# Adaptive norms of a second transformer stack, taken by row tile: factors multiplied in by a product with their diagonal, and the next sublayer's first products started on tile 0

## The chip, the cores and the metric

One core of a Trainium2 chip runs the whole program in one launch. The metric is the device time of that launch in microseconds (us), as the median of three runs. TensorE is called PE in the profile, VectorE DVE, ScalarE ACT, GpSimd POOL, and SyncE (which issues the loads) SP.

## The reference

Two stacks of transformer layers run one after the other on one sequence of 256 tokens and 1024 features, in fp32. The first stack (two layers of f1, m, f2, with plain norms) ends in a norm of its own. The second stack (two layers of F1, M, F2) is the one at issue. Its norms are "adaptive": each of the six sublayers has a shift, a scale and a gain of its own, computed from a condition vector.

```python
def _rms_norm(x, g):
    y = x * lax.rsqrt(jnp.mean(x * x, axis=-1, keepdims=True) + 1e-6)
    return y * g

def _modulate(x, shift, scale):
    return x * (1.0 + scale) + shift

# second stack, layer l: F1, M, F2
n = _modulate(_rms_norm(h, norm_g[l, 0]), sh1, sc1)
h = h + 0.5 * ga1 * _swiglu(n, ffn_w_in[l, 0], ffn_w_out[l, 0])
n = _modulate(_rms_norm(h, norm_g[l, 1]), sh2, sc2)
h = h + ga2 * _token_mixing(n, ...)
n = _modulate(_rms_norm(h, norm_g[l, 2]), sh3, sc3)
h = h + 0.5 * ga3 * _swiglu(n, ffn_w_in[l, 1], ffn_w_out[l, 1])
# after both layers
return _rms_norm(h, final_norm_g)
```

The mean of squares runs over the 1024 features of a token. So the factor of a token (its row) is known only when both 512-column halves of its row of x are complete.

## The kernel before

**Tiles.** The 256 tokens are two row tiles of 128 (tile 0 and tile 1, `t` in the code), and x is `m.x[:, t, :]`, tokens on the partitions. A product needs the features on the partitions, so x is turned by PE, 128x128 at a time (`turn_x`, L1484), and kept as a high and a low part, `xh` and `xl`. Each weight block is split the same way: ACT rounds it into `wh` (L1755), DVE subtracts to get `wl` (L1999). A product of full accuracy is then three PE products: xh with wh (L1509), xh with wl (L1510), xl with wh (L1512), each 128x512. A "sub" is two 128-row blocks of a weight, so it is 12 products for the two tiles. There are five buffers for split subs (`NH`), three are kept ahead (`LA`), and four raw buffers take the loads. SP issues the load of a raw buffer after the last DVE split of the one that it replaces (`load`).

**Order.** Each engine's instructions are generated by the same walk through one `Order` class, in program order per engine; semaphores tie them. There is no planner. What stands first in the walk stands first in each queue.

**The end of a sublayer.** `into_x` computes the down (or output) projection into x, by halves of 512 columns (`h`). In the last half the two last subs are done by `tail`: 12 products (L1523 to L1525) for tile 0, then 12 for tile 1. DVE multiplies the sum by the gain row `gaB` (L2089) and adds it to x (L2091), ACT squares and sums (`square_part`, L1775). In the FFNs the first half of x is turned 8 products into the second half's work (`prep` at k = 4), in the output projection of M between the two tails.

**The norm of the second stack.** `leave` waits for the squares of both tiles, `scale_part` forms the mean on DVE (L2039, L2041), POOL takes it to the power -1/2 for both tiles at once (`rr`, L2392). Meanwhile the rest of x is turned and multiplied by the feature's factor (`v_hi` on ACT L1789, `v_lo` on DVE L2055). DVE makes `dg`, the diagonal of the token factors (L2063), PE spreads it over all partitions by a product with ones (`spread_rr`, L1552), and then for each of 8 feature blocks DVE multiplies `vT` by the spread factors (L2070), ACT adds the shift into `xh` (L1796), and DVE forms `xl` (L2075). Only then do the next sublayer's products start (`gemm_sub`), both tiles together.

The six places where this happens are called T1 to T6 here: T1 is the entrance to the second stack, after the first stack's final norm (`final`, L2379, and `enter`), then T2 = F1 to M, T3 = M to F2, T4 = F2 to F1, T5 = F1 to M, T6 = M to F2. At the end of all, `final` scales x and `store` writes it out.

Of the kernel before, what the change touches and what calls it, by code (L numbers as in the profile page):

```python
# [12 lines left out]
P = 128  # L13
D = 1024
# [68 lines left out]
LA = 3  # L83
AGE = 3
# [256 lines left out]
class Signals:  # L341
    def __init__(self, sem):
# [6 lines left out]
        self.pow = Sem(sem("s_pow"), "POOL")  # L349
# [19 lines left out]
class Order:  # L369
# [5 lines left out]
    def __init__(self, k, e, count):  # L375
# [3 lines left out]
        self.sub_of = {}  # L379
# [12 lines left out]
        self.set_up = False  # L392

# [188 lines left out]
    def prep_hi(self, p, nx):  # L582
        for n, (k, b, tk) in enumerate(p):
            if nx[0] == "plain":
                done = self.new(self.s.act, "xh")
                self.x_hi_plain(k, b, tk, nx, done)
                self.x_hi[k] = self.x_hi[k + 1] = done
            elif n == 0:
                self.need_ada(nx[1], 4)
                done = self.new(self.s.act, "v")  # L590
                self.v_hi(k, b, tk, nx[1], done)
                self.free[b] = self.v_at[k // 2] = done
# [4 lines left out]
    def v_hi(self, k, b, tk, s, done):  # L597
        pass

    def prep_lo(self, p, nx):  # L600
        for n, (k, b, tk) in enumerate(p):
            if nx[0] == "plain":
                done = self.new(self.s.vec, "xl")
                self.x_lo_plain(k, b, nx, self.x_hi[k], done)
                self.free[b] = self.x_lo[k] = self.x_lo[k + 1] = done
            elif n == 1:
                done = self.new(self.s.vec, "v")
                self.v_lo(k, b, tk, nx[1], done)
                self.free[b] = self.v_at[k // 2] = done
# [4 lines left out]
    def v_lo(self, k, b, tk, s, done):  # L614
        pass

    def finish(self, nx):
        s = nx[1]
        b = self.next_t()
        self.spread_rr(s, b)  # L620
        for k in range(9):
            if k < 8:
                self.shifted_hi(s, k, b)
            if k > 0:
                self.shifted_lo(s, k - 1)
# [4 lines left out]

    def spread_rr(self, s, b):
        pass

    def shifted_hi(self, s, k, b):
        pass

    def shifted_lo(self, s, k):
        pass

    def enter(self, nx):  # L640
        mod = nx[0] == "mod"
        if mod:
            for h in range(2):
                for t in range(2):
                    self.square(t, h)
            self.row_scale()
        self.prep(0, nx)
        self.prep(1, nx)
        if mod:
            self.finish(nx)  # L650
        self.ahead()
        if not mod:
            for h in range(2):
                for t in range(2):
                    self.square(t, h)
            self.row_scale()

    def leave(self, nx, bb):
        if nx is not None and nx[0] == "plain":
            p = self.prep_turn(1, bb)  # L660
            self.prep_hi(p, nx)
            self.prep_lo(p, nx)
            self.square(1, 1)
            self.row_scale()
            return
# [18 lines left out]
    def into_x(self, label, banks2, X, K, ready, ga, nx, hook, start=None, td=None):  # L684
        turned, p = nx is None, None
        for h in range(2):
            b, k = start[h] if start else (banks2(), 0)
            end = K if h == 0 else max(k, K - 4)
            while k < end:
# [3 lines left out]
                if h == 1 and k == 4 and not turned:  # L693
                    self.prep(0, nx)
                    turned = True
            if h == 0:
# [7 lines left out]
                continue  # L704
            two = [self.take(label) for _ in range((K - k) // 2)]
            self.ahead()
            for t in range(2):
# [1848 lines left out]
```

## Time and profile before

| | |
|---|---|
| median of 3 runs | 2398.83 us (2398.77 to 2399.57) |
| the profiled execution | 2399.14 us, its span 2397.1 us |
| PE busy | 2283.8 us (95%), 10872 instructions |
| DVE busy | 1578.8 us (66%) |
| ACT busy | 1130.4 us (47%) |
| POOL busy | 19.7 us (1%), 26 instructions |
| mean granted PE clock | 0.981 |

The span runs from the first to the last instruction, and the execution takes 2.0 us more than it. "Busy" of PE is modelled and overlaps (a 128x512 product is shown with 0.39 us and the next starts 0.23 us later), so 95% is not 95% of what PE can do. The granted clock is 1.00 when TensorE runs at its full 2.4 GHz and 0.50 at 1.2 GHz.

### The profile page before, as it was taken

What the parts mean: (1) busy time and instruction counts of PE and PEld (TensorE: products, weight loads), DVE (VectorE), ACT (ScalarE), POOL (GpSimd) and SP (SyncE); (2) the same over time, 40 slices, a digit from 0 to 9 for tenths busy, and PEclk for the clock granted to TensorE, in tenths of its full rate; (3) what the DMA queues carried; (4) which work ended last, traced back from release to release, by engine and by line L of the source; (5) the groups of instructions that cost most, each with busy time, mean ns of one, the idle gap of its engine ahead of it and who ended that gap; (6) DMA issues with size and microseconds to landing.
All of it is one profiled execution on the core that took longest, in us unless ns stands there. A gap on an engine that the chain in (4) does not pass through costs nothing.

```text
span 2397.1 us, 27023 instructions
## 1 busy us (share of the span) xinstructions
PE 2283.8 (95%) x10872; PEld 1903.9 (79%) x10872; DVE 1578.8 (66%) x2391; ACT 1130.4 (47%) x1707; POOL 19.7 (1%) x26
## 2 busy tenths in 40 slices
PE   7999899999999899989999999899999999998998
PEld 6888778888888788868887877788787778777887
DVE  4556775555557669967985545689689955447565
ACT  4445444444444444454444555444444445554443
POOL 0000000000000000000000000000000000000000
PEclk9999999999999999989999999999999999998999
DMA  7554445555554358847874433488589844335563
GB/s 256 192 186 150 124 128 196 176 193 177 201 175 125 121 187 296 294 162 264 305 261 141 128 123 123 158 298 293 199 282 304 290 139 137 123 106 180 199 209 123
DMA packets 250385, 462.91 MB, mean 193 GB/s; under 512 B 9543, under 2 KB 55537, under 8 KB 250133
## 3 DMA queue, kind: packets, MB, share of 16 engines
q1 hardware_dynamic: 250020, 461.04, 57.6%
q8 instruction: 85, 1.39, 0.2%
q14 instruction: 40, 0.32, 0.0%
q10 hardware_dynamic: 240, 0.16, 0.0%
HBM read 460.12 MB, written 1.05 MB: 192 GB/s over the span
## 4 chain that ended last, share of the span: by engine, by line
PE 73%; DVE 13%; issue 9%; ACT 3%; POOL 0%; DMA 0%; ACTq 0%; DVEq 0%; POOLq 0%
PE ps L1509 15%; PE ps L1512 15%; PE ps L1510 15%; PE s L1512 6%; PE s L1509 5%; PE s L1510 5%; DVE wl L1999 4%; PE ps L1484 3%; DVE acc L2007 3%; DVE cacc L2185 2%; PE s L1570 2%; PE ps L1590 1%; ACT wh L1755 1%; PE ps L1525 1%; PE ps L1523 1%
## 5 line engine op out<-in xcount | busy, mean ns | idle before, releaser
L1999 DVE TENSOR_TENSOR wl<-raw,wh 128x1024 fp32r<-128x1024 f32 (+1 forms) x748 | 861.7, 1176 | 397.0 <-ACT wh L1755 391.9
L1755 ACT ACTIVATE wh<-raw 128x1024 fp32r<-128x1024 f32 (+1 forms) x748 | 742.7, 1019 | 342.3 <-PE ps L1512 235.5
L1509 PE MATMUL ps<-wh,xh 128*128 128x512 f32 (+3 forms) x1728 | 671.9, 389 | 18.3 <-DVE wl L1999 11.8
L1512 PE MATMUL ps<-wh,xl 128*128 128x512 f32 (+3 forms) x1728 | 654.5, 379 | 0.0
L1510 PE MATMUL ps<-wl,xh 128*128 128x512 f32 (+3 forms) x1728 | 654.1, 379 | 0.0
L1509 PEld LDWEIGHTS ps<-wh,xh 128*128 128x128 f32 x1728 | 329.4, 191 | 92.3 <-DVE wl L1999 17.8
L1512 PEld LDWEIGHTS ps<-wh,xl 128*128 128x128 f32 x1728 | 329.0, 190 | 53.1 <-DVE xl L2075 0.4
L1510 PEld LDWEIGHTS ps<-wl,xh 128*128 128x128 f32 x1728 | 330.0, 191 | 48.9
L2007 DVE SCALAR_TENSOR_TENSOR acc<-raw,condT,acc 128x512 f32<-128x512 f32 x252 | 189.3, 751 | 7.7
L1509 PE MATMUL s<-wh,xh 128*128 128x512 f32 x384 | 150.3, 391 | 1.9 <-DVE wl L1999 1.9
L1512 PE MATMUL s<-wh,xl 128*128 128x512 f32 x384 | 149.6, 390 | 0.0
L1510 PE MATMUL s<-wl,xh 128*128 128x512 f32 x384 | 149.4, 389 | 0.0
L1509 PE MATMUL s<-wh,hTh 128*128 128x512 f32 x352 | 138.5, 393 | 0.0
L1512 PE MATMUL s<-wh,hTl 128*128 128x512 f32 x352 | 137.3, 390 | 0.0
L1510 PE MATMUL s<-wl,hTh 128*128 128x512 f32 x352 | 137.2, 390 | 0.0
L1761 ACT ACTIVATE ach<-acc 128x512 fp32r<-128x512 f32 x36 | 22.7, 632 | 211.0 <-DVE acc L2007 199.0
L2111 DVE TENSOR_TENSOR hTl<-ps,hTh 128x512 fp32r<-128x512 f32 x88 | 56.9, 685 | 94.8 <-ACT hTh L1812 94.8
L1812 ACT ACTIVATE hTh<-ps 128x512 fp32r<-128x512 f32 x88 | 48.3, 593 | 141.7 <-PE ps L1484 141.6
L1509 PE MATMUL ps<-wh,hTh 128*128 128x512 f32 x288 | 112.6, 391 | 0.0
L1512 PE MATMUL ps<-wh,hTl 128*128 128x512 f32 x288 | 112.1, 389 | 0.0
L1510 PE MATMUL ps<-wl,hTh 128*128 128x512 f32 x288 | 112.0, 389 | 0.0
L1819 ACT ACTIVATE pt<-pt,small 128x128 f32<-128x128 f32 (+1 forms) x88 | 42.0, 478 | 141.5 <-DVE small L2119 141.5
(311 smaller groups left out, 2480.1 us busy)
## 6 DMA issues: line engine op xcount, KB each, us to landing
raw<-in_ffn_w_in SPq DMA_DIRECT2D x80, 1024.0 KB, 5.3
raw<-in_ada_w SPq DMA_DIRECT2D x72, 1024.0 KB, 5.2
raw<-in_ffn_wg SPq DMA_DIRECT2D x40, 1024.0 KB, 5.2
raw<-in_ffn_wu SPq DMA_DIRECT2D x40, 1024.0 KB, 5.2
raw<-in_ffn_wd SPq DMA_DIRECT2D x40, 1024.0 KB, 5.2
raw<-in_ffn_w_out SPq DMA_DIRECT2D x40, 1024.0 KB, 5.3
raw<-in_mix_w_in SPq DMA_DIRECT2D x28, 1024.0 KB, 5.1
raw<-in_w_in SPq DMA_DIRECT2D x28, 768.0 KB, 4.5
```

What stands on the lines that cost most here:

```text
L1484: return self.e.transpose(out, src, self.m.ident[0:n, 0:n])
L1509: e.matmul(o, X[0](kk, t), hi, start=kk == 0, stop=False)
L1510: e.matmul(o, X[0](kk, t), lo, start=False, stop=False)
L1512: ins = e.matmul(o, X[1](kk, t), hi, start=False, stop=kk == K - 1)
L1570: ins = self.e.matmul(m.s45[:, o:o + w], q, k, start=True, stop=True)
L1755: ins = self.e.activation(m.wh[j % NH][:, 0:n], m.raw[u % NR][:, k0 * w:k0 * w + n], ACT.Copy)
L1812: self.then_inc(self.e.activation(m.hTh[:, k:k + 2, :].rearrange("p k s -> p (k s)"), m.ps[b], ACT.Copy), th)
L1819: self.then_inc(self.e.activation(d, d, ACT.Exp, bias=st.sm[:, t:t + 1], scale=-1.0, accum_out=st.sm[:, 4 + t:5 + t]), sgm["exp"])
L1999: ins = self.e.tensor_tensor(m.wl[j % NH][:, 0:n], m.raw[u % NR][:, k0 * w:k0 * w + n], hi, ALU.subtract)
L2007: ins = self.e.scalar_tensor_tensor(out=a, in0=m.raw[u % NR][:, k * 512:k * 512 + 512], scalar=m.condT[:, kk:kk + 1], in1=a if kk else m.b ...
L2111: self.then_inc(self.e.tensor_tensor(lo, m.ps[b], hi.bitcast(F32), ALU.subtract), tl)
L2185: ins = e.scalar_tensor_tensor(out=a, in0=src, scalar=w, in1=a, op0=ALU.mult, op1=ALU.add)
```

## The change

1. The tail takes three subs instead of two where x leads to an adaptive norm or to a final norm (`TAIL`), so 18 products for tile 0, then 18 for tile 1. After M the tail stays at two subs.
2. Each tile has a norm of its own: squares, `scale_part` (one DVE instruction in place of two, the division by 1024 now sits in the scale of the square) and the power on POOL run for one tile.
3. x isn't turned by a transpose and multiplied afterwards. `scaled_part` multiplies a 128x128 block of x with the tile's `dg`, which turns it and applies the token's factor in one plain fp32 product. Eight such products per tile; no spread, no `L2070`.
4. The feature's factor and the shift are applied together while PSUM is read, per 128x128 block: to `xh` directly (ACT) and to `vT` (ACT or DVE), then `xl` is `vT` minus `xh`.
5. `skewed` runs the first 8 x 2 blocks (four subs) of the next sublayer's first projection by tile: tile 0's 24 products, with tile 1's gain, add, squares, norm and turn beside or between them, then tile 1's 24 products.
6. Four subs must be split before the norm. One of the low parts is taken by POOL (`split_lo_pool`), on a semaphore of its own.
7. The transposes in the FFN's second half and between M's tails go away. The first stack's final norm and the last one also go by tile, and each tile is stored on its own.

```diff
+TAIL = 3
...
+    def lower(self, pool=False):
+        j, u, k0, nk, w, last = self.later.pop(0)
+        if pool:
+            self.lo_at[j] = (self.s.plo, j)
+            self.split_lo_pool(j, u, k0, nk, w)
+        else:
+            self.lo_at[j] = (self.s.lo, j)
+            self.split_lo(j, u, k0, nk, w)
+        if last:
+            self.load(u + NR, self.lo_at[j], self.lo_at[j - 1] if k0 else None)
...
+    def skewed(self, label, banks):
+        nx, add_1 = self.half
+        s = nx[-1]
+        while self.wsub < self.taken + 4:
+            self.make(later=True)
+        v0 = self.turn_scaled(s, 0, (self.next_t(), self.next_t()))
+        add_1(lambda: self.shifted_v(s, 0, 2, v0))
+        self.shifted_hi(s, 0, 0, v0)
+        self.shifted_hi(s, 0, 1, v0)
+        self.square(1, 1)
+        if len(self.later) > 1:
+            self.lower()
+        self.lower(pool=True)
+        self.shifted_v(s, 0, 3, v0)
+        self.shifted_hi(s, 0, 2, v0)
+        self.shifted_hi(s, 0, 3, v0)
+        self.normed(1, nx)
+        self.shifted_v(s, 0, 0, v0)
+        self.shifted_v(s, 0, 1, v0)
+        js = [self.take(label) for _ in range(4)]
+        x = {k: (s, 0, k // 2) for k in range(8)}
+        self.first_hi(js, banks[0], x)
+        self.shifted_lo(s, 0, 2)
+        if nx[0] == "mod":
+            v1 = self.turn_scaled(s, 1, (4, 5))
+        for p in (0, 1, 3):
+            self.shifted_lo(s, 0, p)
+        self.first_lo(js, banks[0], x)
+        if nx[0] == "final":
+            v1 = self.turn_scaled(s, 1, (4, 5))
...
+        self.first_rest(js, banks[1])
+        self.ahead()
...
-            end = K if h == 0 else max(k, K - 4)
+            end = K if h == 0 else max(k, K - (4 if plain else 2 * TAIL))
...
+    def scaled_part(self, s, t, bb, tk):
+        m = self.m
+        self.wait_ge(*(self.xr[t, h] for h in range(2)), (self.s.vec, ("dg", s, t)))
+        for k in range(8):
+            b = bb[k // 4]
+            self.wait_ge(self.free[b])
+            ins = self.e.matmul(m.ps[b][:, (k % 4) * P:(k % 4 + 1) * P], m.x[:, t, k * P:(k + 1) * P],
+                                m.dg[:, t * P:(t + 1) * P], start=True, stop=True)
+            if k % 4 == 3:
+                self.then_inc(ins, tk[k // 4])
...
+    def split_lo_pool(self, j, u, k0, nk, w):
...
+        ins = self.e.tensor_tensor(m.wl[j % NH][:, 0:n], m.raw[u % NR][:, k0 * w:k0 * w + n], hi, ALU.subtract)
+        self.then_inc(ins, (s.plo, j))
```

PE at T2, before: the last product of tile 1's tail, the transposes of x's second half, the spread of the factors, and the first products of M's first projection (`wh` and `xh` are high parts).

```order
L1525 MATMUL ps<-wh_61,hTl 128x512
L1484 MATMUL s<-cst,x 128x128 [waits s_vec]
L1484 MATMUL s<-cst,x 128x128 x3
L1484 MATMUL s<-cst,x 128x128 [waits s_vec]
L1552 MATMUL ps<-dg,cst 128x256 [waits s_act,s_vec]
L1509 MATMUL ps<-wh_57,xh 128x512 [waits s_act]
L1510 MATMUL ps<-wl_62,xh 128x512
L1512 MATMUL ps<-wh_57,xl 128x512 [waits s_vec]
```

PE at T2, now: tile 1's last product, the scaled turn of tile 0 (L1651), tile 0's products with `xh` (L1664, L1667, L1671), the scaled turn of tile 1, tile 0's products with `xl` (L1683) and tile 1's (L1694 and on).

```order
L1621 MATMUL ps<-wh_61,hTl 128x512
L1651 MATMUL ps<-dg,x 128x128 [waits s_vec]
L1651 MATMUL ps<-dg,x 128x128 x7
L1664 MATMUL ps<-wh_57,xh 128x512 [waits s_act,s_hi]
L1664 MATMUL ps<-wh_59,xh 128x512 [waits s_act]
L1664 MATMUL ps<-wh_60,xh 128x512 [waits s_act]
L1671 MATMUL ps<-wl_64,xh 128x512 [waits s_lo]
L1651 MATMUL s<-dg,x 128x128 [waits s_vec]
L1683 MATMUL ps<-wh_57,xl 128x512 [waits s_vec]
L1681 MATMUL ps<-wl_65,xh 128x512 [waits s_plo]
L1683 MATMUL ps<-wh_60,xl 128x512 [waits s_vec]
L1694 MATMUL ps<-wh_57,xh 128x512 [waits s_act]
```

The spread is gone, the products with `xh` stand ahead of those with `xl`, and the second tile's turn stands between them.

DVE at T2, now: from tile 0's gain to tile 1's diagonal.

```order
L2232 TENSOR_TENSOR ps<-ps,gaB_75 128x512 [waits s_prod]
L2241 TENSOR_TENSOR x<-ps,x 128x512 [waits s_vec]
L2195 SCALAR_TENSOR_TENSOR ms<-ssq 128x1 [waits s_act]
L2210 TENSOR_SCALAR dg<-cst,rr 128x128 [waits s_pow]
L2232 TENSOR_TENSOR ps<-ps,gaB_75 128x512 [waits s_sub]
L2219 TENSOR_SCALAR vT<-ps,Gc_83,shc_81 128x128 [waits s_turned]
L2241 TENSOR_TENSOR x<-ps,x 128x512 [waits s_vec]
L2155 TENSOR_TENSOR wl_64<-raw_56,wh_59 128x1024 [waits s_hi]
L2219 TENSOR_SCALAR vT<-ps,Gc_83,shc_81 128x128 x2
L2195 SCALAR_TENSOR_TENSOR ms<-ssq 128x1 [waits s_act]
L2227 TENSOR_TENSOR xl<-vT,xh 128x2x128 [waits s_act,s_vec]
L2210 TENSOR_SCALAR dg<-cst,rr 128x128 [waits s_pow]
```

Before, both gains and adds stood in a row and one mean, one power and one pair of diagonals followed. Now tile 1's gain and add stand behind tile 0's diagonal, with a read of tile 0's turned x between them.

POOL, now, around T1 and T2 (two powers per tile at T1, since the final norm takes one too).

```order
L2549 TENSOR_TENSOR rr<-ms,cst 128x2 [waits s_vec]
L2549 TENSOR_TENSOR rr<-ms,cst 128x1 [waits s_vec] x2
L2543 TENSOR_TENSOR wl_64<-raw_54,wh_59 128x1024 [waits s_hi]
L2549 TENSOR_TENSOR rr<-ms,cst 128x1 [waits s_vec] x3
L2543 TENSOR_TENSOR wl_65<-raw_56,wh_60 128x1024 [waits s_hi]
```

Before, POOL's queue here held powers alone. Now the split of a sub stands between tile 0's power and tile 1's, six times in all.

## Rows read from the trace of the kernel before

**Rows 1.** Stretches: us, busy of PE, PEld, DVE, ACT, POOL, granted clock, DMA share
```profile
1057.50:1070.60 13.10, 5.07 (x19) 3.26 (x18) 6.53 (x16) 5.74 (x16) 1.39 (x2) 0.65 0.01 1
1070.60:1075.50 4.90, 4.90 (x12) 3.88 (x13) 4.83 (x13) 3.33 (x8) 0.00 (x0) 0.54 0.00 0
1263.30:1269.20 5.90, 1.94 (x11) 1.06 (x9) 3.55 (x9) 1.97 (x6) 0.69 (x1) 1.00 0.71 187
1269.20:1273.40 4.20, 4.16 (x11) 3.22 (x12) 4.18 (x12) 2.84 (x6) 0.00 (x0) 0.59 0.88 241
1523.10:1531.30 8.20, 3.13 (x11) 1.63 (x10) 6.14 (x14) 2.84 (x8) 0.69 (x1) 0.66 0.40 130
1531.30:1536.20 4.90, 4.90 (x12) 3.88 (x13) 4.83 (x13) 3.32 (x8) 0.00 (x0) 0.53 0.00 0
1724.40:1730.20 5.80, 1.82 (x11) 0.94 (x9) 3.56 (x10) 2.00 (x6) 0.69 (x1) 1.00 0.00 0
1730.20:1734.10 3.90, 3.89 (x10) 3.03 (x11) 3.90 (x11) 2.54 (x6) 0.00 (x0) 0.56 0.02 4
1931.50:1937.80 6.30, 2.30 (x11) 1.11 (x9) 3.58 (x10) 2.02 (x6) 0.69 (x1) 0.80 0.75 213
1937.80:1942.40 4.60, 4.60 (x11) 3.68 (x12) 4.60 (x13) 3.03 (x7) 0.00 (x0) 0.53 0.60 166
2192.20:2200.40 8.20, 3.24 (x11) 1.64 (x10) 6.15 (x13) 2.83 (x8) 0.69 (x1) 0.65 0.59 194
2200.40:2205.10 4.70, 4.68 (x11) 3.71 (x12) 4.70 (x13) 3.12 (x7) 0.00 (x0) 0.52 0.00 0
```

**Rows 2.** Chain of waits: one 128x512 product, and eight transposes, start us and us
```profile
1260.50 0.23 PE ps L1525
...
1199.77 0.87 PE ps L1484 x8
```

**Rows 3.** Timeline of T2: start us, us, what, and the idle time before it
```profile
1263.48 0.70 DVE L2089 TENSOR_TENSOR ps<-ps,gaB 128x512 f32<-128x512 f32 x1 [1.30 <-PE ps L1525]
...
1264.95 0.63 ACT L1775 ACTIVATE junk<-x 128x512 f32<-128x512 f32 x1 [2.00 <-DVE x L2091]
1266.21 0.69 POOL L2392 TENSOR_TENSOR rr<-ms,cst 128x2 f32<-128x2 f32 x1 [200.60 <-DVE ms L2041]
1266.94 0.48 DVE L2063 TENSOR_SCALAR dg<-cst,rr 128x128 f32<-128x128 f32 x2 [0.22 <-POOL rr L2392]
1269.24 0.50 PE L1509 MATMUL ps<-wh,xh 128*128 128x512 f32 x1 [1.05 <-ACT xh L1796]
```

**Rows 4.** Groups of instructions by shape: count, busy us, mean ns of one
```profile
L1999 DVE TENSOR_TENSOR wl<-raw,wh 128x1024 fp32r<-128x1024 f32 x632 | 755.7, 1222 | 326.2 <-ACT wh L1755 321.4
L2353 DVE SCALAR_TENSOR_TENSOR zt<-ps,cq,cst 128x128 f32<-128x128 f32 x12 | 4.2, 351 | 8.3 <-PE ps L1712 8.3
L1876 ACT ACTIVATE zt<-ps 128x128 f32<-128x128 f32 x12 | 3.3, 274 | 21.6 <-PE ps L1642 21.6
```

**Rows 5.** Timeline: a run of plain fp32 products of 128 columns, 32 records for 16 products
```profile
1296.73 3.65 PE L1664 MATMUL ps<-w1b,ptT 128*15 128x128 f32 x32
```

**Rows 6.** Timeline of T3: two splits, and the gain of tile 0 behind them
```profile
1521.43 2.36 DVE L1999 TENSOR_TENSOR wl<-raw,wh 128x1024 fp32r<-128x1024 f32 x2 [1.74 <-ACT wh L1755]
1523.71 0.69 DVE L2089 TENSOR_TENSOR ps<-ps,gaB 128x512 f32<-128x512 f32 x1
```

**Rows 7.** Timeline of the end: the final scaling of four halves, 2.74 us
```profile
2391.82 2.74 DVE L2379 SCALAR_TENSOR_TENSOR x<-x,rr,gaB 128x512 f32<-128x512 f32 x4 [0.81 <-POOL rr L2392]
```

**Rows 8.** Stretches of the mixing layers with short gaps on PE, columns as rows 1
```profile
321.10:324.50 3.40, 2.24 (x13) 1.66 (x12) 2.97 (x7) 0.79 (x2) 0.00 (x0) 0.96 0.18 24
324.50:327.90 3.40, 3.40 (x11) 2.84 (x11) 1.61 (x2) 1.55 (x2) 0.00 (x0) 0.54 0.80 284
...
1317.70:1321.10 3.40, 2.44 (x15) 2.12 (x13) 2.82 (x12) 1.99 (x4) 0.00 (x0) 1.00 0.01 3
```

**Rows 9.** Timeline of POOL: a power of eight numbers per partition
```profile
315.14 1.63 POOL L2399 TENSOR_TENSOR small<-small,cst 128x8 f32<-128x8 f32 x1 [101.81 <-DVE small L2214]
```

More of the change, by code:

```diff
@@ L392, in __init__ @@
         self.set_up = False
+        self.half = None
     def new(self, sem, name):
@@ L434, in take, with ahead, make @@
         return j, hs, nk, un["w"]
-    def ahead(self):
-        while self.wsub < self.taken + LA and self.made < len(self.k.w.subs):
+    def ahead(self, n=LA):
+        while self.wsub < self.taken + n and self.made < len(self.k.w.subs):
             self.make()
-    def make(self):
+    def make(self, later=False):
         subs = self.k.w.subs
@@ L449, in make @@
             self.sub_of[j] = (j % NH, nk, un)
-            self.split(j, u, k0, nk, un["w"])
-            if last:
-                self.load(u + NR, (self.s.lo, j))
+            self.split_hi(j, u, k0, nk, un["w"])
+            self.later.append((j, u, k0, nk, un["w"], last))
+            if not later:
+                self.lower()
             return
@@ L582, in prep_hi @@
     def prep_hi(self, p, nx):
[L583 to L592, printed above, removed]
+        for k, b, tk in p:
+            done = self.new(self.s.act, "xh")
+            self.x_hi_plain(k, b, tk, nx, done)
+            self.x_hi[k] = self.x_hi[k + 1] = done
@@ L658, in leave @@
-    def leave(self, nx, bb):
[L659 to L665, printed above, removed]
+        for h in range(2):
+            for t in range(2):
+                self.square(t, h)
+        self.row_scale()
+    def leave(self, nx, bb):
+        p = self.prep_turn(1, bb)
+        self.prep_hi(p, nx)
+        self.prep_lo(p, nx)
@@ L692, in into_x @@
                 hook(h, k)
-                if h == 1 and k == 4 and not turned:
+                if h == 1 and k == 4 and plain:
                     self.prep(0, nx)
@@ L703, in into_x, with add_1 @@
                     self.square(t, 0)
[L704 to L707, printed above, removed]
[L708 to L716 removed]
+        if not plain and nx[-1] is not None:
+            self.need_ada(nx[-1], 4)
+        two = [self.take(label) for _ in range((K - k) // 2)]
+        self.ahead(LA if plain else NH - len(two))
+        first, last = (self.s.prod, ("tail", two[0][0])), (self.s.sub, two[-1][0])
+        self.x_sum = last
+        self.tail(0, two, b[0], X, k, K, ready)
+        if plain and not turned:
+            p = self.prep_turn(0, (self.next_t(), self.next_t()))
+        self.add_x(0, 1, b[0], first, ga)
+        if p:
+            self.prep_hi(p, nx)
+        self.square(0, 1)
+        self.tail(1, two, b[1], X, k, K, ready)
+        if plain:
+            self.add_x(1, 1, b[1], last, ga)
             if p:
                 self.prep_lo(p, nx)
[L719 to L720 removed]
+            self.leave(nx, b0)
+            return
+        self.normed(0, nx)
+        def add_1(between=lambda: None):
+            self.add_x(1, 1, b[1], last, ga, between)
+        if nx[-1] is not None:
+            self.half = nx, add_1
+            return
+        add_1()
+        self.square(1, 1)
+        self.normed(1, nx)
     def tail(self, t, two, b, X, k, K, ready):
```

364 lines of the change are left out of this document (210 added, 154 removed).

## The prediction

> **What bounds the kernel now.** PE does, except at the places where it has nothing to do. I read the page first, then the stretches around each norm of the second stack, then the timeline inside one of them. Each of the six norms shows the same two costs [rows 1]: a stretch from the end of tile 1's tail to the next sublayer's first product in which PE has next to nothing that must be done, and behind it a stretch in which the granted clock is about half, so 9 to 11 products take 0.43 us each where one takes 0.227 (the row rounds it to 0.23) [rows 2]. T1 has 13.1 us and then 4.9 us at 0.54, T2 5.9 and 4.2 at 0.59, T3 8.2 and 4.9 at 0.53, T4 5.8 and 3.9 at 0.56, T5 6.3 and 4.6 at 0.53, T6 8.2 and 4.7 at 0.52. Of a slow stretch about half is lost: 2.4, 1.9, 2.4, 1.9, 2.3 and 2.4 us. So the excess over the products' own time is 15.5, 7.8, 10.6, 7.7, 8.6 and 10.6, together **60.8 us**. These are the only places where the change can win much. At the end lies one more such chain, closed by 2.74 us of scaling [rows 7].
>
> T2 is one chain [rows 3]: gain at 1263.48 and add, squares at 1264.95, power at 1266.21, diagonals at 1266.94, spread, first shift, first product at 1269.24. At T3 the chain starts later, since tile 0's gain stands behind two splits on DVE [rows 6].
>
> **The change at T2, step by step.** Let 0 be the end of tile 0's tail. All that follows is worked out from rows and program order.
>
> - PE: tile 1's 18 products take 18 x 0.227 = 4.1 us. Meanwhile tile 0's chain runs: gain starts at 0.2, squares 1.47 later at 1.7, power 1.26 later less the 0.2 of the dropped DVE instruction, at 2.7, diagonal at 3.5 to 3.7 [rows 3]. So it is ready when the tail ends. This is the point of the longer tail: with 12 products it would be 1.0 us late.
> - PE: the scaled turn. The trace has no plain fp32 product with 128 moving columns and 128 weights. The nearest are 0.114 us per record, two records each, but with 15 weight columns [rows 5], and a transpose of 128 columns, with the weights changed each time, at 0.109 [rows 2]. I take 0.114 and 16 records: 1.8 us, 4.1 to 5.9. The upper end is 0.227 a record, the price of a 512-column one: 3.6 us.
> - ACT reads it from 5.2, 128 columns each. A plain read takes 0.274 [rows 4]. With scale and bias I estimate 0.3 apart, so the first half of `xh` is there from 5.85 and 6.45, and PE runs 8 products to 7.7 without a wait.
> - DVE: tile 1's gain 4.3 to 5.0, then two reads into `vT` which wait for the second half of the turn, 6.1 to 6.8 (0.351 for such a shape [rows 4]), add to 7.5, ACT's squares to 8.25. Behind the squares ACT copies the third quarter of `xh`, to 8.7. PE waits 1.0 us, then does 2 products. DVE's split (1.22 [rows 4]) and two more reads end at 9.4, the last quarter is copied at 9.85: PE waits 0.7 us and is through with 4 products at 10.8.
> - Tile 1's mean at 9.6, power to 10.3, diagonal 10.6. Its turn 10.8 to 12.6, tile 0's 10 last products to 14.9, tile 1's 24 to 20.3. ACT and DVE have tile 1's parts by 13.9, so there is no wait.
>
> Excess: 20.3 - 4.1 - 48 x 0.227 = **5.3 us**, both turns (3.6) in it. Before it was 7.8, and the 8 transposes in the middle of the second half (0.87 [rows 2]) go as well: **3.4 us won at T2**, 3.3 at T4, 4.2 at T5.
>
> **T3 and T6.** The tail stays at 12 products, and the gain of tile 0 still stands behind two splits (1523.71 [rows 6]). Squares, power and diagonal end 3.5 us later, at 1527.25. The tail now ends at 1522.2, as the 8 transposes before it are gone, so PE idles 5 us and the clock falls as it does now (0.66 in the stretch [rows 1]). The turn then runs at half speed (3.4 us), the first products start at 1530.7 and some 4 of them are slow. By the same steps the last of the 48 ends at 1544.4, against 1531.3 + 10.9 + 2.4 = 1544.6 now. I book **0.2 and 0.3 us**: the chain is as long as it was.
>
> **T1.** Each tile takes two norms. Tile 0's diagonal is ready at 6.4, 2.3 us behind the tail. Worse, tile 1's add stands behind the read of tile 0's turn and its two norms on ACT and DVE end at 16, while ACT's reads of tile 0 into `vT` stand behind tile 1's squares: the `xl` products wait from 13.0 to 16.3. The last of the 48 ends at 26.7, plus about 2.5 for a clock that a gap of 3.2 us costs: excess 14.2, against 15.5. **1.3 us won.**
>
> **The end.** The last chain is the same up to the power, then scales two halves instead of four: 2.74 / 2 = 1.4 less [rows 7], 0.2 for the dropped mean instruction and some 0.3 less because half the stores have gone, but tile 1's gain waits 0.55 for tile 0's scaling. **1.35 us won.**
>
> **POOL's splits.** They cost nothing as long as they end before tile 1's power is wanted, since it is queued behind them. At T2 the split can start at 4.5 (its high part is the last of four on ACT) and the power is wanted at 9.6: 5.1 us of room; at the others 5 to 6. The trace has no such instruction. Below stands 1.22, the same subtraction on DVE [rows 4]; above stands POOL's own rate, (1.63 - 0.69) / 6 = 0.157 us for each further number per partition [rows 3, 9], which for 1024 would be 160 us. That row is a power, this is a subtraction, so I take the DVE row's kind and a few times its price: under 5 us. The Trainium skill (GPSIMD Engine Reference, 3.1 Elementwise) measures 4497 ns for 2048 fp32 numbers per partition, against 2293 on VectorE; by it I estimate 2.3 us here, and the sum would be the same.
>
> **Sum.** 1.3 + 3.4 + 0.2 + 3.3 + 4.2 + 0.3 + 1.35 = 14.0 us. From the profiled execution's 2399.1 this gives **2385 us**; the median of the runs is 0.3 lower, which I leave out. I do not expect the gain to be eaten later: where DVE is the slow one in the FFNs, it works at most three subs ahead of PE, so it starts earlier by the same amount.
>
> **The rivals.**
>
> *The clock falls in the new gaps.* The two gaps of 1.0 and 0.7 us lie within 2.2 us. For it: at 321.1 PE is busy for 2.24 of 3.40 us and the clock is 0.54 in the stretch behind. Against: at 1317.7 it is busy 2.44 of 3.40 and stays at 1.00 [rows 8], and at T2 it is busy only 1.94 of 5.9 and falls just at the end [rows 1]. If it falls at T2, T4 and T5, each loses what a slow stretch costs now, 1.8: 2385 + 5.4 = 2390 us.
>
> *The turn is dearer.* At 0.227 a record, 12 turns cost 12 x 1.8 = 22 us more at most. Against it speak the transposes, whose 128 weight columns are loaded within 0.109. A third of that surcharge gives 2392, all of it 2407.
>
> *POOL takes tile 1's factor hostage (slower).* If a split takes longer than its room of about 5.6 us, each further microsecond is paid six times. The 14 us are used up at 5.6 + 14 / 6 = **7.9 us** a split. At 12 us the kernel takes 2385 + 6 x 6.4 = 2423. For it speaks only POOL's power row [rows 9]; against it, that a subtraction is not a power.
>
> *POOL and DVE hold each other up.* Then each split costs DVE's `ms`, `dg` or split up to its own length. At T2 the DVE instructions during the split (gain, reads, add) take one operand from PSUM, so little should meet; where all six meet a split of twice DVE's price, 6 x 2.4 = 14 us are lost and the time is 2399, no change. The Trainium skill (SBUF — State Buffer, Who interferes with whom) says that a DVE instruction with two SBUF inputs and a GpSimd instruction that reads SBUF exclude each other for the whole instruction; no run here shows it yet, and this rival is that rule.
>
> **Chances.** Forecast 0.55, clock 0.20, dearer turn 0.10, mutual hold 0.07, POOL hostage 0.05, and 0.03 for a loss unseen here. A measurement of this kernel can tell about 0.2%, 4.8 us, from no change. The range goes down to 2377, if T1's clock stays up (2.5), both gaps are shorter (about 1 each at three places) and T3 and T6 win 1 each, and up to 2395, which holds the clock rival and a third of the dearer turn. Faster 0.84, same 0.08 (mutual hold, part of the dearer turn), slower 0.08.
>
> **What would show it.** In the profile after: PE's first `L1664` product within 2 us of the tail's end at T2, T4 and T5; the records of `L1651` at 0.11 apart; gaps of about 1.0 and 0.7 us ahead of the third and fourth `xh` quarter, with the clock at 1.00; POOL's `L2543` at 2 to 3 us and idle time before tile 1's power; T3 and T6 still with 5 us of idle PE. Wrong would be: `L2543` above 5 us, `L1651` above 0.15, or a clock below 0.7 over the first 24 products at T2.

## The result

The changed kernel takes 2384.32 us (median of 4 runs, 2383.75 to 2384.74), the kernel before 2399.20 (4 runs on the same chips). The ratio is 0.9937, with a 95% interval of 0.9919 to 0.9954. The profiled execution took 2384.17 us, the forecast said 2385. The page of the changed kernel begins, with span, busy times and the chain that ended last:

```profile
span 2382.2 us, 27252 instructions
...
PE 2280.7 (96%) x10956; PEld 1906.1 (80%) x10956; DVE 1561.4 (66%) x2367; ACT 1140.4 (48%) x1755; POOL 37.4 (2%) x40
...
PE 78%; DVE 16%; ACT 4%; issue 2%; POOL 0%; DMA 0%; ACTq 0%; DVEq 0%; POOLq 0%
```

PE is busy 3.1 us less in a span that is 14.9 us shorter, so most of the gain is idle time that went. POOL has 18 us more to do, 14 of them in its six splits. One run of the version called "both" below (2676.37 us, granted clock 0.81) and one of the kernel before beside it (7574.72 us, 0.35) ran at a far lower clock than the others and stand in no comparison here.

The stretches that answer to [rows 1], same columns. For T1: from the tail's end to the first product, and the slow stretch further on. For T2 and T3: from the tail's end to the first product, and the 4.2 us behind it.

```profile
1059.00:1063.10 4.10, 2.13 (x17) 1.86 (x16) 0.45 (x2) 3.46 (x7) 2.00 (x2) 1.00 0.00 0
1070.50:1073.90 3.40, 3.40 (x9) 2.70 (x10) 0.96 (x3) 0.16 (x1) 0.00 (x0) 0.57 0.00 0
1261.20:1263.10 1.90, 1.88 (x17) 1.69 (x15) 0.70 (x1) 1.01 (x4) 1.69 (x1) 1.00 0.09 15
1263.10:1267.30 4.20, 3.38 (x13) 2.21 (x14) 3.75 (x9) 2.71 (x9) 1.32 (x2) 1.00 1.00 288
1517.70:1526.00 8.30, 3.47 (x17) 3.37 (x17) 3.94 (x7) 3.07 (x8) 2.89 (x2) 0.67 0.43 130
1526.00:1530.20 4.20, 4.09 (x16) 3.04 (x16) 3.16 (x9) 2.64 (x9) 0.54 (x1) 0.83 0.75 243
```

At T2 the 5.9 us without work have become 1.9, and PE spends them on the scaled turn. The clock is at 1.00 where it was 0.59. T3 is as long as it was: 8.3 us to the first product, clock 0.67 in them.

Rows picked from the timeline of T2 in the changed kernel (start us, us, and in brackets the engine's idle time before it; those between are left out):

```profile
1260.28 0.29 DVE L2210 TENSOR_SCALAR dg<-cst,rr 128x128 f32<-128x128 f32 x1 [0.65 <-POOL rr L2549]
1261.13 1.95 PE L1651 MATMUL ps<-dg,x 128*128 128x128 f32 x16
1261.41 2.36 POOL L2543 TENSOR_TENSOR wl<-raw,wh 128x1024 fp32r<-128x1024 f32 x1 [1.17 <-ACT wh L1900]
1263.17 0.47 PE L1664 MATMUL ps<-wh,xh 128*128 128x512 f32 x1
1264.36 1.21 DVE L2155 TENSOR_TENSOR wl<-raw,wh 128x1024 fp32r<-128x1024 f32 x1
1264.85 0.39 PE L1667 MATMUL ps<-wl,xh 128*128 128x512 f32 x1
1265.56 0.73 PE L1664 MATMUL ps<-wh,xh 128*128 128x512 f32 x2 [0.32 <-ACT xh L1952]
1266.36 0.66 POOL L2549 TENSOR_TENSOR rr<-ms,cst 128x1 f32<-128x1 f32 x1 [2.60 <-DVE ms L2195]
1266.72 0.73 PE L1664 MATMUL ps<-wh,xh 128*128 128x512 f32 x2 [0.43 <-ACT xh L1952]
1267.75 0.49 PE L1651 MATMUL s<-dg,x 128*128 128x128 f32 x3
```

Tile 0's diagonal is there 0.6 us before the tail ends, so the turn starts the moment PE is free. From then on PE has only two short gaps before tile 1's turn. POOL's split ends at 1263.77 and POOL then waits 2.60 us for tile 1's mean.

**Where the 14.9 us come from.** Both kernels issue the same 8832 products of sublayers and tails, so one can look up when the product of the same number starts in each trace and see the distance change from place to place. Measured so, the gain is 2.7 us at T1, 3.4 at T2, 0.1 at T3, 3.3 at T4, 4.3 at T5, 0.4 at T6 and 1.55 behind the start of the last product (9.18 us from there to the end before, 7.63 now): 15.8. Elsewhere 0.9 are lost on balance. The first product starts 0.2 us later in this execution and the first stack is 1.2 us longer, in steps of 0.7, 0.3 and 0.2 where it waits or its clock changes; between the later places 0.6 are won. The changed kernel and the nine versions below, all with the same code in the first stack, spread over 2.0 us in that stretch, so I take the 1.2 for the scatter of one execution.

### The profile page after: what moved, and what is told of

The parts are those of the page before. It is cut to its first block, busy times and chain, and to the rows that moved or that the text cites. A ratio compares the mean times of both kernels' runs of the same rounds, so it can differ in the third digit from the quotient of the medians.

```text
span 2382.2 us, 27252 instructions
## 1 busy us (share of the span) xinstructions
PE 2280.7 (96%) x10956; PEld 1906.1 (80%) x10956; DVE 1561.4 (66%) x2367; ACT 1140.4 (48%) x1755; POOL 37.4 (2%) x40
## 3 DMA queue, kind: packets, MB, share of 16 engines
q8 instruction: 86, 1.41, 0.2%
## 4 chain that ended last, share of the span: by engine, by line
PE 78%; DVE 16%; ACT 4%; issue 2%; POOL 0%; DMA 0%; ACTq 0%; DVEq 0%; POOLq 0%
PE ps L1605 15%; PE ps L1608 15%; PE ps L1606 15%; PE s L1608 6%; PE s L1605 6%; PE s L1606 6%; DVE wl L2155 5%; DVE acc L2163 4%; PE ps L1580 3%; DVE cacc L2335 2%; PE s L1715 2%; PE ps L1735 1%; ACT wh L1900 1%; PE ps L1621 1%; PE ps L1620 1%
## 5 line engine op out<-in xcount | busy, mean ns | idle before, releaser
L2155 DVE TENSOR_TENSOR wl<-raw,wh 128x1024 fp32r<-128x1024 f32 (+3 forms) x742 | 855.3, 1177 | 383.2 <-ACT wh L1900 378.3
L1605 PE MATMUL ps<-wh,xh 128*128 128x512 f32 (+3 forms) x1632 | 628.9, 385 | 11.5 <-DVE wl L2155 11.4
L1608 PE MATMUL ps<-wh,xl 128*128 128x512 f32 (+3 forms) x1632 | 613.5, 376 | 0.0
L1606 PE MATMUL ps<-wl,xh 128*128 128x512 f32 (+3 forms) x1632 | 612.6, 375 | 0.0
L1605 PEld LDWEIGHTS ps<-wh,xh 128*128 128x128 f32 x1632 | 308.7, 189 | 77.4 <-DVE wl L2155 17.4
L1608 PEld LDWEIGHTS ps<-wh,xl 128*128 128x128 f32 x1632 | 308.5, 189 | 47.8
L1606 PEld LDWEIGHTS ps<-wl,xh 128*128 128x128 f32 x1632 | 309.1, 189 | 44.7
L1605 PE MATMUL ps<-wh,hTh 128*128 128x512 f32 x268 | 104.5, 390 | 0.0
L1608 PE MATMUL ps<-wh,hTl 128*128 128x512 f32 x268 | 104.3, 389 | 0.0
L1606 PE MATMUL ps<-wl,hTh 128*128 128x512 f32 x268 | 104.3, 389 | 0.0
```

Source lines behind the costliest of these rows:

```text
L1605: e.matmul(o, X[0](kk, t), hi, start=kk == 0, stop=False)
L1606: e.matmul(o, X[0](kk, t), lo, start=False, stop=False)
L1608: ins = e.matmul(o, X[1](kk, t), hi, start=False, stop=kk == K - 1)
L2155: ins = self.e.tensor_tensor(m.wl[j % NH][:, 0:n], m.raw[u % NR][:, k0 * w:k0 * w + n], hi, ALU.subtract)
```

## The experiments

Each number for a place is the change in distance from the changed kernel, by the same products in the two traces. "Late" is more time than the changed kernel. The kernel before was timed again beside each group of runs, with medians from 2399.2 to 2401.1 us, so a difference between medians of two groups is uncertain by 1 to 2 us; the places come from one execution of each.

| | T1 | T2 | T3 | T4 | T5 | T6 | span |
|---|---|---|---|---|---|---|---|
| before | 2.7 | 3.4 | 0.1 | 3.3 | 4.3 | 0.4 | +14.9 |
| split on DVE | 2.2 | 1.1 | 0.7 | 1.1 | 1.1 | 1.0 | +9.9 |
| POOL's split three times | 3.5 | 5.0 | 0.6 | 5.6 | 3.7 | 1.0 | +18.5 |
| tail of 12 | 2.8 | 1.0 | 0.0 | 1.0 | 1.0 | 0.0 | +9.8 |
| no early products | 3.8 | 4.5 | 4.2 | 5.4 | 5.1 | 4.7 | +26.9 |
| turn twice | 4.0 | 3.6 | 4.0 | 3.6 | 3.6 | 3.8 | +22.2 |
| M's splits late | 0.0 | 0.0 | -4.5 | 0.0 | 0.0 | -4.1 | -7.4 |
| T1's order | -4.0 | 0.0 | 0.0 | 0.0 | 0.0 | 0.3 | -4.3 |
| both | -4.0 | 0.0 | -4.4 | 0.0 | 0.0 | -4.1 | -11.6 |
| both, kept apart | -4.5 | -0.3 | -5.1 | -0.3 | -0.3 | -4.7 | -16.1 |

What is missing to the span lies between the places, where the last section comes to it, and behind the last product (1.55 us for the kernel before, 1.4 for the tail of 12, nothing for the others).

### Which part of the change wins: no early products

```diff
+        v1 = self.turn_scaled(s, 1, (4, 5))
         self.first_hi(js, banks[0], x)
...
-            v1 = self.turn_scaled(s, 1, (4, 5))
```

> The turn by the diagonals stays, but tile 0's first products wait behind tile 1's turn, so PE has nothing between the two turns. My theory (the gain comes from the products that fill the wait for tile 1's factor, not from the shorter way of applying the factors): at T2, T4, T5 the second turn waits until 1267.45, ends at 1269.3 and 48 products follow: 2.9 us more than the change each; T1 1.9, T3 and T6 4.7 each. Sum 20 us, 2404, and 26 us, 2410, if the clock falls at T2, T4 and T5 as well, which I hold for likely since PE then idles 4 us there. So slower than the kernel before. Rival (the gain is mostly the shorter chain: no spread, no scaled, no shift one by one): 5 to 8 us more than the change, 2390 to 2392, still faster than before.

It took 2411.04 us, ratio to before 1.0046 (1.0031 to 1.0061): slower than the kernel before. The second turn at T2, and the stretch that holds it:

```profile
1270.88 3.65 PE L1648 MATMUL s<-dg,x 128*128 128x128 f32 x16 [4.30 <-DVE dg L2207]
```

```profile
1270.00:1273.40 3.40, 2.52 (x12) 2.55 (x13) 1.72 (x5) 2.10 (x7) 0.41 (x1) 0.65 1.04 289
```

PE idles 4.30 us and then turns at half the clock, 3.65 us where 1.95 are needed. So the turn by the diagonals, with the longer tail, the norms by tile and POOL's splits beside it, is worth nothing without the early products. What wins is that PE has tile 0's products to do while tile 1's factor is made, and keeps its clock through them. The sum was 27 us, near the expected 26.

### What the turn costs: turn twice

```diff
+            for _ in range(2):
                 ins = self.e.matmul(m.ps[b][:, (k % 4) * P:(k % 4 + 1) * P], m.x[:, t, k * P:(k + 1) * P],
```

> Each of the 16 records of a scaled turn is run twice into the same place (same result), so 12 turns have 16 records more each. My theory (both turns lie on PE's path, 0.114 us a record at full clock and 0.23 where the clock is down, which is at T3's and T6's first turn): 10 x 1.8 + 2 x 3.6 = 25 us more than the change, 2409. Rival (at T2, T4, T5 PE waits for tile 1's factor anyway, so a longer first turn is hidden): about 6 us less, 2403. Rival (a record costs 0.227 in truth and the 1.95 us of the first look is the pipelining of something else): 40 us more, 2425.

2406.47 us, ratio 1.0028 (1.0017 to 1.0040). T2's first turn:

```profile
1263.76 3.73 PE L1652 MATMUL ps<-dg,x 128*128 128x128 f32 x32
```

At T2, T4 and T5 two doubled turns cost 3.57 us, that is 0.112 a record, and all of it is late: no part of a turn is hidden. T3 and T6 cost 3.9 instead of the expected 5.4, so only a part of the added records ran at the low clock. The "dearer turn" of the forecast is out, and so is the rival that PE waits for tile 1's factor anyway.

### The longer tail: tail of 12

```diff
-TAIL = 3
+TAIL = 2
```

with the splits ahead of the tail kept at the FFNs' two.

> The tail of the FFNs back from 18 to 12 products a tile; M's is 12 anyway. My theory: tile 0's sum is complete 1.36 us later, its diagonal is ready 0.9 to 1.0 us after the tail's end instead of 0.5 before it, so T2, T4 and T5 (two of them behind F1 and one behind F2) lose 0.9 each, T1 1.4, the end 0 to 0.3: about 4.2 us, 2388.5; the clock stays at 1.00 at T2, T4, T5. Rival 1 (the longer tail does nothing since tile 1's chain sets the second turn): less than 1.5 us in all. Rival 2 (the extra idle microsecond ahead of the first turn brings the clock down): 1.8 us more at each of three places, 2394.

2393.66 us, ratio 0.9973 (0.9963 to 0.9984). T2's first turn now waits:

```profile
1264.19 2.02 PE L1651 MATMUL ps<-dg,x 128*128 128x128 f32 x16 [0.78 <-DVE dg L2210]
```

The idle time in brackets is counted from the modelled end of a product (0.39 us), not from where the next could start (0.227), so the wait is 0.94 us. T2, T4 and T5 lose 1.0 each, as worked out, with the clock up. T1 lost 2.8, twice the 1.4 expected: its first turn took 3.13 us in a low stretch of clock which the change doesn't have. Of the remaining 4 us, 1.4 are at the end, where 0.3 at most was expected, the others between the places. So the total is 5 us above the 2388.5 that I expected, and the longer tail's own price is read from T2, T4 and T5 alone.

### What POOL's split saves: split on DVE

```diff
-        self.lower(pool=True)
+        self.lower()
```

> POOL's split goes back to DVE, 1.22 us each, the rest of the change stays. My theory (POOL's split is hidden, and what it saves is 1.2 us of DVE on the path of tile 0's last reads and of tile 1's mean): at each of T1 to T6 the last quarter of xh, tile 1's power and the second turn come 1.2 us later, so about 6 x 1.2 = 7 us more than the change, 2391.5 us, PE's gap ahead of the last quarter at T2 about 1.6 us instead of 0.4, and the clock at T2 still 1.00. Rival 1 (DVE has room there): no difference, 2384. Rival 2 (a gap of 1.6 us in 5 us brings the clock down): T2, T4 and T5 lose 1.8 more each, 2397 us, with 0.5 to 0.6 granted in the products behind the second turn. Rival 3 (mutual hold of DVE and POOL costs something in the change): less than 7 us more, with gain, add and reads of DVE shorter than in the change while POOL's split ran.

2393.74 us, ratio 0.9972 (0.9963 to 0.9981). T2, DVE's splits and the gap on PE ahead of the last quarter of `xh`:

```profile
1266.09 2.35 DVE L2155 TENSOR_TENSOR wl<-raw,wh 128x1024 fp32r<-128x1024 f32 x2
...
1269.59 0.73 PE L1664 MATMUL ps<-wh,xh 128*128 128x512 f32 x2 [1.56 <-ACT xh L1952]
```

The gap is 1.56, 1.6 were expected, and T2, T4 and T5 are 1.1 late each. The sum over the six places is 7.2, as my theory had it, if unevenly (2.2 at T1, 0.7 at T3). The clock did not fall at T2 with gaps of 0.33 and 1.56 us. The stretch with the longer gap and the one behind it (columns as rows 1):

```profile
1266.60:1270.00 3.40, 1.51 (x6) 0.66 (x5) 2.96 (x7) 1.52 (x6) 0.66 (x1) 1.00 1.06 291
1270.00:1273.40 3.40, 3.40 (x25) 3.10 (x24) 2.19 (x7) 2.61 (x8) 0.00 (x0) 1.00 1.05 308
```

So at this place the forecast's clock rival is out, with a gap that is longer than the ones it was about. "DVE has room there" is out too, and so is a price of the mutual hold in the change: DVE's gain and first two reads take 0.70 and 0.73 us at T2 with POOL's split beside them or without it.

### How much room POOL has, and the mutual hold: the split three times

```diff
+        for i in range(3):
             ins = self.e.tensor_tensor(m.wl[j % NH][:, 0:n], m.raw[u % NR][:, k0 * w:k0 * w + n], hi, ALU.subtract)
+            if i < 2:
+                self.then_inc(ins, (s.plo, ("again", j, i)))
+                self.wait_ge((s.plo, ("again", j, i)))
```

> POOL makes each of its six splits three times one after the other (the same result), about 7.1 us instead of 2.36. In the change the split starts 4.95 us before tile 1's power at T2, T4 and T5, 4.7 at T1, 6.4 at T3 and 6.05 at T6. My theory (power queued behind the split, nothing else): the power starts 2.1 us later at T2, T4, T5, the second turn had 0.3 us in hand, so 1.8 each; 2.4 at T1; nothing to 0.4 at T3 and T6. Sum 8 us, 2392.5. Rival 1 (mutual hold): DVE's own split, which now falls into POOL's, takes more than its 1.22 us, up to 3 us or more, and the sum is 15 us or more, 2400. Rival 2 (the clock falls in the gap of about 2 us ahead of the second turn): 1.8 more at T2, T4, T5, 2398 us. Rival 3 (POOL is off every path): no difference.

2404.92 us, ratio 1.0019 (1.0010 to 1.0028). I expected 8 us late, it was 18.5 in the span. T2 by the timeline, POOL, DVE and PE:

```profile
1262.60 8.14 POOL L2544 TENSOR_TENSOR wl<-raw,wh 128x1024 fp32r<-128x1024 f32 x3 [1.17 <-ACT wh L1900]
1270.83 0.66 POOL L2553 TENSOR_TENSOR rr<-ms,cst 128x1 f32<-128x1 f32 x1
...
1265.55 2.97 DVE L2155 TENSOR_TENSOR wl<-raw,wh 128x1024 fp32r<-128x1024 f32 x1
1269.08 1.67 DVE L2195 SCALAR_TENSOR_TENSOR ms<-ssq 128x1 f32<-128x1 f32 x1
...
1269.66 1.22 PE L1664 MATMUL ps<-wh,xh 128*128 128x512 f32 x2 [2.18 <-ACT xh L1952]
1271.87 3.79 PE L1651 MATMUL s<-dg,x 128*128 128x128 f32 x16
```

DVE's split takes 2.97 us instead of 1.21 and its mean, one number per partition, 1.67 instead of 0.15; the mean ends at 1270.75, when POOL's third split ends. In between DVE's split ends at 1268.52, and that third split takes 3.22 us instead of 2.36. Each waits for the other's whole instruction. DVE's reads of the turn and its add, with one operand in PSUM, keep their time (0.73 and 0.68) beside POOL's split. So the mutual hold is real: of the 5.0 us at T2 POOL's queue explains 2, the rest is DVE held up, and then the second turn at half the clock. The Trainium skill (SBUF — State Buffer, Who interferes with whom) says that a DVE instruction with two SBUF inputs and a GpSimd instruction that reads SBUF block each other for the whole instruction, and that one with at most one SBUF input does not, outside VectorE's 2-port modes; this trace agrees on both, by the 1.67 and 3.22 us and by the 0.73 and 0.68 us above.

In the changed kernel the six splits happen to lie beside DVE instructions of the second kind. That, and not the absence of the rule, is why the change did not pay for it. The one trace of it there is on POOL's power of one number, 0.66 us instead of 0.54 where it starts beside DVE's two-operand `xl`, as at T2.

### The two places where nothing was won: M's splits late

```diff
-        self.ahead(LA if plain else NH - len(two))
+        late = not plain and label == "wo2"
+        if late:
+            while self.wsub < self.taken + 2:
+                self.make(later=True)
+        else:
+            self.ahead(LA if plain else NH - len(two))
...
         self.square(0, 1)
+        if late:
+            while self.wsub < self.taken + 3:
+                self.make(later=True)
...
-        add_1(lambda: self.shifted_v(s, 0, 2, v0))
+        def between():
+            while len(self.later) > 2:
+                self.lower()
+            self.shifted_v(s, 0, 2, v0)
+        add_1(between)
```

`make(later=True)` makes only ACT's high part; DVE's subtraction follows behind tile 1's gain. T3 of the changed kernel, and of this one:

```profile
1516.92 2.36 DVE L2155 TENSOR_TENSOR wl<-raw,wh 128x1024 fp32r<-128x1024 f32 x2 [1.74 <-ACT wh L1900]
1519.20 0.69 DVE L2232 TENSOR_TENSOR ps<-ps,gaB 128x512 f32<-128x512 f32 x1
...
1522.66 3.75 PE L1651 MATMUL ps<-dg,x 128*128 128x128 f32 x16 [4.83 <-DVE dg L2210]
```

```profile
1514.72 0.70 DVE L2244 TENSOR_TENSOR ps<-ps,gaB 128x512 f32<-128x512 f32 x1
...
1518.43 2.02 PE L1663 MATMUL ps<-dg,x 128*128 128x128 f32 x16 [1.03 <-DVE dg L2222]
```

> At T3 and T6 alone: the two weight splits which DVE makes ahead of tile 0's gain go behind tile 1's gain, and ACT makes one of their high parts behind tile 0's squares. My theory (T3 and T6 are long only because tile 0's gain stands behind those splits): tile 0's gain starts at 1515.2 instead of 1519.20, the diagonal is ready at 1518.5 instead of 1522.22, PE's idle time before the first turn falls from 4.8 to about 1 us, and the clock stays up in most of the stretch: 5 us won at each, 2374.5. Rival 1 (the splits are wanted by the first products, so the idle time moves behind the turn): 1 to 2 us at each, 2381. Rival 2 (PE waits so briefly but the clock falls all the same): 3 us at each, 2378. Rival 3 (loads are issued later, since each is released by a split, and a later sub comes late): nothing won, 2384 to 2386.

2377.04 us, ratio 0.9904 (0.9888 to 0.9919), 7.3 us less than the change. The gain starts 4.5 us earlier, PE's idle time falls from 4.83 to 1.03 us, and the turn takes 2.02 instead of 3.75 us, so the clock stays up. T3 wins 4.5 and T6 4.1 where 5 were expected. So T3 and T6 were long for the reason that the forecast read from [rows 6], and it was no loss of the change but a gain left lying. The splits do meet POOL's: its own takes 3.22 us there instead of 2.36.

### T1's order

```diff
+        if nx[0] == "final" and nx[-1] is not None:
...
+            self.final(n, 0)
+            add_1()
+            for t, h in ((0, 0), (0, 1), (1, 1)):
+                self.square(t, h)
+            self.row_scale(0, 1)
```

and in `skewed`, for T1, tile 1's first mean, power and scaling ahead of the reads of tile 0, its second mean behind them, and tile 1's turn ahead of the products with `xl`.

> At T1 alone: tile 1's last add goes ahead of tile 0's second mean on DVE instead of behind the reads of tile 0's turn, ACT reads tile 0 into vT ahead of tile 1's second squares' end, the split goes behind, and tile 1's turn goes ahead of the products with xl as at the other places. My theory (T1 is long because tile 1's two norms begin only 5 us after its tail's end): tile 1's diagonal is ready at about 1067 instead of 1071.4, the last of the 48 products ends 5.5 us earlier at T1, 2379 us. Rival 1 (ACT is the bound at T1: reads, squares and copies of both tiles queue there): 1 to 2 us, 2383. Rival 2 (clock falls as now, since PE idles around the first turn as before): 3.5 us, 2381.

2380.01 us, ratio 0.9919 (0.9901 to 0.9936). T1 wins 4.0 of the expected 5.5, and its low stretch of clock is gone. In the chain to tile 1's diagonal two instructions are longer than alone, DVE's scaling of tile 1 and POOL's last power. The rows of DVE's scaling, POOL's split and that power:

```profile
1061.19 3.57 DVE L2558 SCALAR_TENSOR_TENSOR x<-x,rr,gaB 128x512 f32<-128x512 f32 x2 [0.65 <-POOL rr L2579]
...
1061.18 2.37 POOL L2573 TENSOR_TENSOR wl<-raw,wh 128x1024 fp32r<-128x1024 f32 x1
...
1066.19 1.79 POOL L2579 TENSOR_TENSOR rr<-ms,cst 128x1 f32<-128x1 f32 x1 [2.64 <-DVE ms L2225]
```

Two scalings take 1.42 us elsewhere. Here they start with POOL's split and stand still until it ends. The power takes 0.54 to 0.55 us alone; here DVE's split starts at 1066.03, just before it, and the power is 1.2 us longer. Which of the two costs how much of the missing 1.5 us, this run doesn't tell.

### Both together, and then kept apart

> The two edits together, splits late at T3 and T6 and the order at T1. They touch different places, so the gains add: 5 x 2 + 5.5 us, 2369. Rival (the stretches of low clock move with the phase of the program, some 0.9 us each, as the products from 1790 to 1903 us cost 1.7 us more in two experiments than in the change with the same instructions): within 4 us of that sum either way.

2371.47 us (median of three runs; 2372.03 with the one named in the first section), ratio 0.9883 (0.9866 to 0.9901). Place by place the gains are those of the two edits alone (4.0, 4.4 and 4.1). They are 12.5 of the expected 15.5 us, and the median lies 2.5 us above the expected 2369.

The last kernel is meant to keep POOL's and DVE's two-operand instructions apart. At T1 both splits are DVE's, behind its reads; elsewhere the read goes ahead of the split:

```diff
-            self.lower(pool=True)
             self.shifted_hi(s, 0, 0, v0)
...
+            self.shifted_v(s, 0, 3, v0)
             if len(self.later) > 1:
                 self.lower()
             self.lower(pool=True)
-            self.shifted_v(s, 0, 3, v0)
```

> e8_both, with POOL's and DVE's instructions that read two operands from SBUF kept apart: at T1 both splits are DVE's, behind its reads of tile 0, and at T2 to T6 DVE reads the last two blocks ahead of its split instead of behind it. In e8_both DVE's two scalings at T1 take 3.56 us where two take 1.42 elsewhere, and POOL's split ran from 1061.08 to 1063.45. My theory (DVE stood still until POOL's split ended): the pair takes 1.42 again, tile 1's second squares and the reads start 2.1 us earlier, and T1 gives 2 us less excess. At T2, T4 and T5 the gap ahead of the last quarter of xh (0.4) goes and the second turn starts 0.4 earlier, at T3 and T6 0.8 of gap becomes about 0.3. Sum 2 + 3 x 0.4 + 2 x 0.4 = 4 us less than e8_both, 2368. Rival (the scalings take 3.56 for a reason of their own, ACT's squares reading x beside them for one): T1 stays, and it is 2370.

2368.75 us, ratio 0.9868 (0.9852 to 0.9885). T1 by the timeline:

```profile
1061.08 1.42 DVE L2569 SCALAR_TENSOR_TENSOR x<-x,rr,gaB 128x512 f32<-128x512 f32 x2 [0.66 <-POOL rr L2590]
1062.56 1.36 DVE L2260 TENSOR_SCALAR vT<-ps,Gc,shc 128x128 f32<-128x128 f32 x4
1064.92 2.35 DVE L2196 TENSOR_TENSOR wl<-raw,wh 128x1024 fp32r<-128x1024 f32 x2
...
1065.08 1.46 POOL L2590 TENSOR_TENSOR rr<-ms,cst 128x1 f32<-128x1 f32 x1 [4.04 <-DVE ms L2236]
1067.86 2.05 PE L1692 MATMUL s<-dg,x 128*128 128x128 f32 x16 [0.93 <-DVE dg L2251]
```

The scalings take 1.42 us again, so the hold was their cause; ACT's squares were not, since in the version "both" the first of them starts only at 1064.04, behind POOL's split. But T1 wins only 0.5 more, not 2. Tile 1's factor is there 1.3 us earlier (1066.54 instead of 1067.88 us), but DVE's two splits now stand ahead of tile 1's diagonal, which is ready only 0.4 earlier. POOL's power is still held by DVE's split, 1.46 us where it was 1.79 in "both". At T3 and T6 POOL's split still meets one of DVE's and takes 3.2 us. T3 and T6 win 0.7 and 0.6, T2, T4 and T5 0.3 each: 2.6 us over the six places where 4 were expected. This is the fastest version: 1.3% less than the kernel before, and by the spans of the profiled executions 16.1 us less than the change.

## Why the prediction was right

By its own terms, forecast and measured: T1 1.3 and 2.7, T2 3.4 and 3.4, T3 0.2 and 0.1, T4 3.3 and 3.3, T5 4.2 and 4.3, T6 0.3 and 0.4, the end 1.35 and 1.55. The sum was 14.0, the places gave 15.8 and the span 14.9. The mechanism came out at every place; that the total is as near as 0.9 us is in part luck, since T1's extra 1.4 us were partly offset by the 0.9 lost outside the places, which the forecast did not have.

- **T2.** With the end of tile 0's tail at 1257.05, the diagonal was ready at 3.5 (said 3.5 to 3.7), the first product at 6.1 (5.85), the third quarter of `xh` at 8.5 (8.7), the last at 9.7 (9.85), tile 1's diagonal at 10.3 (10.6), the second turn at 10.7 (10.8), and the last of the 48 products ended at 20.2 (20.3). The two gaps are 0.5 and 0.7 us by the starts of products; the brackets show 0.32 and 0.43 because of the modelled ends. Said were 1.0 and 0.7.
- **The scaled turn.** 0.114 a record from [rows 5] held: 1.95 us for 16 records with the last one's latency, 0.112 each by the doubled turn.
- **T1** was mis-sized, by 1.4 us. The `xl` products of tile 0 started at 15.6 instead of 16.3, and the low clock cost 1.4 us (9 products in 3.40 us at 0.57, which take 2.0 at full clock) where 2.5 were booked. These two make 1.8; the last of the 48 products ended at 27.6 instead of 29.2, and the 0.2 to 0.3 us between are not traced. Its order was read right, as the run with T1's order shows.
- **T3 and T6** came out as worked out, T3 with 11.35 us of excess against 1544.4 - 1522.2 - 10.9 = 11.3, and the run that moves the splits shows that the cause was the one named.
- **The end** (start us, us): the power's two users are now a chain of two tiles.

```profile
2373.94 1.41 DVE L2528 SCALAR_TENSOR_TENSOR x<-x,rr,gaB 128x512 f32<-128x512 f32 x2 [0.66 <-POOL rr L2549]
2375.27 0.69 DVE L2232 TENSOR_TENSOR ps<-ps,gaB 128x512 f32<-128x512 f32 x1
...
2378.29 1.41 DVE L2528 SCALAR_TENSOR_TENSOR x<-x,rr,gaB 128x512 f32<-128x512 f32 x2 [0.66 <-POOL rr L2549]
```

  The last scaling is 1.41 instead of 2.74 us [rows 7], as booked.
- **POOL's split** took 2.36 us, near the 2.3 that the forecast derived from the Trainium skill (GPSIMD Engine Reference, 3.1 Elementwise), and far from the 160 that POOL's power row would have given. The room was 4.95 us at T2 (said 5.1). But the break-even of 7.9 us a split was too generous: for three splits in a row, 7.1 us, its rule gives 2385 + 6 x 1.5 = 2394, and 2404.9 was measured. It left out that a long split also holds DVE and is held by it: the three took 8.14 us at T2.
- **The rivals.** The clock did not fall in the gaps, nor with 1.56 us in the run with the split on DVE; with the split three times, behind a gap of 2.18, the second turn took 3.79 us. The dearer turn is excluded. The mutual hold is real and cost the change next to nothing only because of what lies beside the splits; it made DVE's two scalings 2.1 us longer in the run with T1's order. The forecast gave it 0.07 for the right reason, that the DVE instructions beside the split take an operand from PSUM.

## What to carry to other kernels

When a factor comes late in a norm, look for work that needs only the rows that are ready: the gain here is tile 0's 14 products that fill the wait for tile 1's factor, and the same kernel without them was slower than the one before. A queue that does something not yet wanted ahead of a chain's first step, as DVE's two splits at T3 and T6, can cost its full length and the clock behind it; moving them won 8.6 us at the two places, 7.3 by the medians. In these runs work given to POOL was free beside DVE instructions with an operand in PSUM and not beside those with two from SBUF: check what each DVE instruction during it reads.

## What the runs showed that I had not expected

**The same instructions, with and without a low stretch of clock.** The part of F1 from about 1790 to 1903 us has the same instructions in the changed kernel and in all experiments. In five of them (split on DVE, tail of 12, turn twice, M's splits late, both) it takes 1.5 to 1.7 us more. Stretches there, of the version with both edits and of the one kept apart (columns as rows 1):

```profile
1806.40:1809.80 3.40, 1.56 (x8) 0.98 (x7) 3.33 (x6) 3.40 (x5) 0.00 (x0) 1.00 1.02 363
1809.80:1813.20 3.40, 3.40 (x10) 2.65 (x9) 3.29 (x5) 1.71 (x3) 0.00 (x0) 0.55 0.61 191
```

```profile
1804.10:1807.50 3.40, 1.54 (x8) 0.97 (x7) 3.33 (x6) 3.40 (x5) 0.00 (x0) 1.00 1.02 368
1807.50:1810.90 3.40, 3.40 (x16) 2.78 (x17) 3.29 (x5) 1.94 (x4) 0.00 (x0) 1.00 0.67 186
```

PE has the same idle time (busy 1.56 and 1.54 of 3.40), and behind it the clock is 0.55 in one and 1.00 in the other. The instructions are the same, and what differs in these rows is the moment at which they come. There are two such places in this F1, and in the M behind T5 three of the runs (split on DVE, POOL's split three times, tail of 12) took 1.5 to 1.8 us more in the same way. So an edit elsewhere can cost or win 0.8 us at each such place, and I would not trust a sum of terms below some 2 to 3 us. What decides at a given moment was not tested.

**POOL and DVE hold each other in both directions**, down to instructions of one number per partition: 0.15 became 1.67 us on DVE (the split three times), 0.55 became 1.79 (T1's order, both) and 1.46 (kept apart) on POOL.
